# Block two makes all its own low parts, in a new order of projections and attention

## The reference

```python
h = rms_norm_2(x, attn_norm_g[l])
proj = h @ w_in[l]                       # 1024 x 3656
(mq, mk, mv, dq, dk, dv, sq, sk, sv, iq, ik, iw) = jnp.split(proj, offsets, axis=-1)
moba = moba_attention(qk(mq), qk(mk), mv)          # 4 heads, causal here
diff = diff_attention(dq 1 and 2, dk 1 and 2, dv, lam)   # 4 heads, v twice as wide
diff = rms_norm_2(diff, diff_subln_g[l]) * (1.0 - lam_init)
dsa = dsa_attention(qk(sq), qk(sk), sv, rope(iq), rope(ik), iw)   # 4 heads
x = x + concat(moba, diff, dsa) @ w_out[l]
h2 = rms_norm_2(x, ffn_norm_g[l])
x = x + (silu(h2 @ w_gate[l]) * (h2 @ w_up[l])) @ w_down[l]
```

## Time and profile before

| | us |
|---|---|
| three runs | 1736.86, 1734.09, 1737.43 |
| median | 1736.86 |
| profiled execution | 1736.14 |
| its span | 1734.0 |
| TensorE busy | 1622.6 |
| VectorE busy | 1048.5 |
| ScalarE busy | 760.5 |

### The profile page before, as it was taken

The page is one execution under the profiler, slowest core; times in us unless marked ns, Lnnn a source line. Parts: engine busy times, 40 slices in busy tenths (PEclk is TensorE's granted clock), DMA queues, the critical chain, the costliest instruction groups (busy, mean ns, idle before and its releaser), DMA issues.

```text
span 1734.0 us, 23510 instructions
## 1 busy us (share of the span) xinstructions
PE 1622.6 (94%) x9246; PEld 1319.6 (76%) x9246; DVE 1048.5 (60%) x1599; ACT 760.5 (44%) x1278; POOL 112.4 (6%) x120
## 2 busy tenths in 40 slices
PE   6999999999999989989999998789999998799999
PEld 3865676787888877578988866579998766589997
DVE  3537654654664346666654566658884566668873
ACT  3435523543453224545544445435454455445442
POOL 1010000010000001000000111100000011100000
PEclk9999999999999989999999999889999999899999
DMA  9349323687772225747655774135555664145553
GB/s 360 114 140 318 109 91 118 204 295 247 278 262 97 86 73 148 245 160 257 179 191 185 232 233 160 62 98 182 183 184 192 213 206 146 51 133 183 182 185 119
DMA packets 193549, 307.93 MB, mean 178 GB/s; under 512 B 12753, under 2 KB 96737, under 8 KB 193313
## 3 DMA queue, kind: packets, MB, share of 16 engines
q1 hardware_dynamic: 186720, 283.86, 49.9%
q0 software_dynamic: 6496, 22.51, 3.7%
q10 hardware_dynamic: 224, 0.07, 0.0%
HBM read 288.62 MB, written 17.78 MB: 177 GB/s over the span
## 4 chain that ended last, share of the span: by engine, by line
PE 79%; DVE 11%; ACT 3%; issue 2%; DMA 2%; POOL 1%; SPq 0%; POOLq 0%; DVEq 0%; ACTq 0%
PE bank L1824 48%; PE pair_bank L1824 20%; PE bank L1884 2%; DVE w_lo L1330 1%; PE pair_bank L2065 1%; PE bank L2093 1%; DVE wide L1414 1%; PE bank L2076 1%; DMA raw<-in_w_ada 1%; ACT probs L1160 1%; POOL xrstd L901 1%; DVE neg_max L1646 1%; DVE variance L1474 1%; POOL rstd L867 1%; PE pair_bank L2111 1%
## 5 line engine op out<-in xcount | busy, mean ns | idle before, releaser
L1330 DVE TENSOR_TENSOR w_lo<-raw,w_hi 128x1024 fp32r<-128x1024 f32 x374 | 448.6, 1220 | 296.5 <-ACT w_hi L1022 294.2
L1022 ACT CAST w_hi<-raw 128x1024 fp32r<-128x1024 f32 (+1 forms) x406 | 417.9, 1044 | 387.6 <-PE bank L1824 300.6
L1824 PE MATMUL pair_bank<-act_hi,w_hi 128*128 128x256 f32 (+1 forms) x736 | 231.1, 314 | 11.6 <-DVE act_lo L1404 6.0
L1824 PE MATMUL pair_bank<-act_hi,w_lo 128*128 128x256 f32 (+1 forms) x736 | 227.6, 309 | 0.0
L1824 PE MATMUL pair_bank<-act_lo,w_hi 128*128 128x256 f32 (+1 forms) x736 | 227.5, 309 | 0.0
L1824 PE MATMUL bank<-w_hi,hid_hi 128*128 128x512 f32 x560 | 222.1, 397 | 3.9 <-DVE residual L1725 3.9
L1824 PE MATMUL bank<-w_hi,hid_lo 128*128 128x512 f32 x560 | 222.0, 396 | 0.0
L1824 PE MATMUL bank<-w_lo,hid_hi 128*128 128x512 f32 x560 | 221.8, 396 | 0.0
L1824 PE MATMUL bank<-w_hi,act_hi 128*128 128x512 f32 (+2 forms) x528 | 212.0, 402 | 4.2 <-DVE w_lo L1330 2.1
L1824 PE MATMUL bank<-w_lo,act_hi 128*128 128x512 f32 (+2 forms) x528 | 203.9, 386 | 0.0
L1824 PE MATMUL bank<-w_hi,act_lo 128*128 128x512 f32 (+2 forms) x528 | 203.2, 385 | 0.0
(11 more groups left out here) (230 smaller groups left out, 2149.2 us busy)
## 6 DMA issues: line engine op xcount, KB each, us to landing
raw<-in_w_mlp SPq DMA_DIRECT2D x128, 512.0 KB, 3.8
raw<-in_w_in SPq DMA_DIRECT2D x106, 512.0 KB, 4.5
raw<-in_w_ada SPq DMA_DIRECT2D x96, 512.0 KB, 5.7
raw<-in_w_gate SPq DMA_DIRECT2D x44, 512.0 KB, 3.5
raw<-in_w_up SPq DMA_DIRECT2D x44, 512.0 KB, 3.5
raw<-in_w_down SPq DMA_DIRECT2D x44, 512.0 KB, 3.5
raw<-in_w_out SPq DMA_DIRECT2D x32, 512.0 KB, 3.9
split_lo<-w_lo POOLq DMA_DIRECT2D x30, 512.0 KB, 4.6
```

The costliest lines, as they stand in the source:

```text
L1022: nc.scalar.copy(hi_of(i)[:, 0:w], raw[:, i % RAW, 0:w]).then_inc(hi_ready, 1)
L1330: nc.vector.tensor_tensor(w_lo[:, i % RAW, 0:w], raw[:, i % RAW, 0:w], hi_of(i)[:, 0:w].bitcast(F32), ALU.subtract).then_inc(lo_ready, 1)
L1824: ins = nc.tensor.matmul(o, a[x], b[y], start=first and i == 0, stop=True, skip_group_check=True)
```

## The change

- The early slots and all that belongs to them are gone: 32 loads, casts, subtractions and stores in the first MLP, 32 reloads in block two, SyncE's waits ahead of them. All 29 low parts of a layer are made in block two by VectorE.
- The eight column blocks are in the order dq, dk, iq, mv_ik, mqk, sqk, dv, sv (before: iq, mv_ik, dq, dk, dv, mqk, sqk, sv). The values of the differential heads come in slots 23 to 26.
- The differential attention steps are scored and weighed from step 11 on. Their mixes wait for dv and are put off to step 28 and the first list of w_out; their transposed weights are kept, each in a place of its own (`MIX_AT`). Moba's mixes come before them, those of dsa all together in the fifth list of w_out.
- VectorE's part of `logits` is an item of its own, `gather`, one step or more behind TensorE's part. The index logits are at steps 16 to 21 instead of 7 to 13, the search is at 21 to the first list of w_out instead of 14 to the third.
- The slots of w_out go in the order of k (0, 2, 4, 6) instead of 2, 4, 0, 6. The differential rows are turned in bank 7 instead of bank 2, in the third list of w_out instead of the first.

```diff
-EARLY_SLOTS = (1, 3, 5, 8, 10, 12, 14, 15, 17, 18, 20, 21, 23, 24, 26, 28)
-EARLY_AT, EARLY_EVERY, BEHIND = 10, 1, 3
-EARLY = [(l, s) for l in range(DEPTH) for s in EARLY_SLOTS]
...
-        BLOCKS2 = (("iq", IQ), ("mv_ik", IK), ("dq", DQ), ("dk", DK), ("dv", DV), ("mqk", MQ), ("sqk", SQ), ("sv", SV))
+        BLOCKS2 = (("dq", DQ), ("dk", DK), ("iq", IQ), ("mv_ik", IK), ("mqk", MQ), ("sqk", SQ), ("dv", DV), ("sv", SV))
...
         FILL2 = {
             1: [("tables",)], 2: [("lam",)],
             3: [("drain", 0, 0), ("drain", 0, 1)],
-            4: [("first", 0), ("second", 0)],
-            5: [("first", 1), ("second", 1), ("turn", 0)],
-            6: [("drain", 1, 0), ("drain", 1, 1), ("turn", 1)],
-            7: [("first", 2), ("second", 2), ("index_scale",), ("turn", 2), ("logits", 0)],
-            8: [("logits", 1)],
-            9: [("logits", 2)],
-            10: [("drain", 2, 0), ("drain", 2, 1), ("logits", 3)],
-            11: [("first", 3), ("logits", 4)],
-            12: [("second", 3), ("first", 4), ("turn", 3)],
-            13: [("second", 4), ("turn", 4), ("logits", 5)],
-            14: [("drain", 3, 0), ("drain", 3, 1), ("search", 0, 3)],
-            15: [("first", 5), ("search", 0, 1)],
-            16: [("second", 5), ("first", 6), ("turn", 5)],
-            17: [("second", 6), ("turn", 6), ("score", 0)],
-            18: [("drain", 4, 0), ("weigh", 0), ("drain", 4, 1), ("search", 0, 2), ("score", 1)],
-            19: [("weigh", 1), ("mix", 0), ("search", 0, 2), ("score", 2)],
-            20: [("weigh", 2), ("mix", 1), ("search", 1, 1), ("score", 3)],
-            21: [("weigh", 3), ("mix", 2), ("search", 1, 1), ("score", 4)],
-            22: [("drain", 5, 0), ("weigh", 4), ("mix", 3), ("drain", 5, 1), ("score", 5)],
-            23: [("weigh", 5), ("mix", 4), ("first", 7), ("score", 6)],
-            24: [("weigh", 6), ("mix", 5), ("second", 7), ("square", 0), ("first", 8), ("turn", 7), ("score", 7)],
-            25: [("weigh", 7), ("mix", 6), ("second", 8), ("turn", 8), ("norm", 0), ("score", 8)],
-            26: [("drain", 6, 0), ("weigh", 8), ("mix", 7), ("drain", 6, 1), ("search", 1, 1), ("score", 9)],
-            27: [("weigh", 9), ("mix", 8), ("first", 9), ("square", 1), ("score", 10)],
-            28: [("drain", 7, 0), ("weigh", 10), ("mix", 9), ("drain", 7, 1), ("second", 9), ("first", 10), ("norm", 1), ("turn", 9), ("score", 11)],
+            4: [("first", 0)],
+            5: [("second", 0), ("first", 1), ("turn", 0)],
+            6: [("second", 1), ("turn", 1)],
+            7: [("drain", 1, 0), ("drain", 1, 1)],
+            8: [("first", 2)],
+            9: [("second", 2), ("first", 3), ("turn", 2)],
+            10: [("second", 3), ("turn", 3)],
+            11: [("drain", 2, 0), ("drain", 2, 1), ("score", 0)],
+            12: [("weigh", 0), ("score", 1), ("first", 4), ("second", 4)],
+            13: [("turn", 4), ("weigh", 1), ("score", 2), ("first", 5), ("second", 5)],
+            14: [("turn", 5), ("drain", 3, 0), ("weigh", 2), ("drain", 3, 1), ("score", 3)],
+            15: [("weigh", 3), ("score", 4), ("first", 6), ("second", 6), ("index_scale",)],
+            16: [("turn", 6), ("weigh", 4), ("score", 5), ("logits", 0)],
+            17: [("weigh", 5), ("score", 6), ("gather", 0), ("logits", 1)],
+            18: [("drain", 4, 0), ("weigh", 6), ("drain", 4, 1), ("score", 7), ("gather", 1), ("logits", 2)],
+            19: [("weigh", 7), ("gather", 2), ("logits", 3), ("first", 7)],
+            20: [("gather", 3), ("logits", 4), ("second", 7), ("first", 8)],
+            21: [("turn", 7), ("gather", 4), ("logits", 5), ("second", 8), ("search", 0, 1)],
+            22: [("drain", 5, 0), ("turn", 8), ("drain", 5, 1), ("score", 8), ("gather", 5), ("search", 0, 3)],
+            23: [("weigh", 8), ("score", 9), ("first", 9)],
+            24: [("mix", 8), ("weigh", 9), ("score", 10), ("second", 9), ("search", 0, 2)],
+            25: [("mix", 9), ("turn", 9), ("weigh", 10), ("score", 11), ("first", 10), ("search", 0, 2)],
+            26: [("drain", 6, 0), ("mix", 10), ("weigh", 11), ("drain", 6, 1), ("second", 10), ("search", 1, 2)],
+            27: [("mix", 11), ("turn", 10), ("score", 12), ("search", 1, 3)],
+            28: [("mix", 0), ("mix", 1), ("mix", 2), ("mix", 3), ("drain", 7, 0), ("weigh", 12), ("drain", 7, 1), ("score", 13),
+                 ("square", 0), ("search", 1, 2)],
         }
         OUT2 = {
-            0: [("weigh", 11), ("mix", 10), ("second", 10), ("turn_rows", 0), ("turn", 10), ("turn_rows", 1), ("score", 12)],
-            1: [("weigh", 12), ("mix", 11), ("search", 1, 2), ("score", 13)],
-            2: [("weigh", 13), ("search", 1, 3), ("mix", 12), ("score", 14)],
-            3: [("weigh", 14), ("mix", 13), ("score", 15)],
-            4: [("weigh", 15), ("mix", 14)],
-            5: [("mix", 15)],
+            0: [("mix", 4), ("mix", 5), ("mix", 6), ("mix", 7), ("weigh", 13), ("square", 1), ("search", 1, 1), ("score", 14)],
+            1: [("norm", 0), ("weigh", 14), ("norm", 1), ("score", 15)],
+            2: [("turn_rows", 0), ("turn_rows", 1), ("weigh", 15)],
+            4: [("mix", 12), ("mix", 13), ("mix", 14), ("mix", 15)],
         }
-        for x in range(len(EARLY)):
-            FILL["mlp1", 0].setdefault(EARLY_AT + x * EARLY_EVERY, []).append(("early", x))
...
-                return [(0, 2), (0, 4), (1, 2), (1, 4), (0, 0), (1, 0), (0, 6), (1, 6)]
+                return [(0, 0), (1, 0), (0, 2), (1, 2), (0, 4), (1, 4), (0, 6), (1, 6)]
...
+        MIX_AT = ((0, 0), (0, 1), (0, 2), (0, 3), (1, 0), (1, 2), (2, 0), (2, 2),
+                  (3, 0), (3, 2), (4, 0), (5, 0), (3, 0), (3, 2), (4, 0), (5, 0))
...
+            place, first = MIX_AT[j]
+            return (probs_t2[:, place] if place < 4 else mix_more[:, place - 4])[:, first:]
...
-                self.known_low(self.i - BEHIND)
...
-            def known_low(self, i):
-
-                if i < 0 or n.slots[i][0] != "known":
-                    return
-                x, r, u = n.value["known", i], i % RAW, n.slots[i][1]
-                was = n.value["early", x]
-                self.e.wait_ge(lo_stored[was % RAW], 16 * n.at(f"lo_stored{was % RAW}", was))
-                self.e.wait_ge(hi_ready, n.at("hi_ready", i))
-                self.e.dma_start(w_lo[:, r, 0:u].bitcast(F32), split_lo[x, :, 0:u]).then_inc(lo_loaded[r], 16)
-                n.put(f"lo_loaded{r}", i)
...
-            def early(self, x):
-                i = n.value.get(("early", x), 0)
-                u = n.slots[i][1]
-                self.e.wait_ge(lo_ready, n.at("lo_ready", i))
-                self.e.dma_start(split_lo[x, :, 0:u], w_lo[:, i % RAW, 0:u].bitcast(F32)).then_inc(lo_stored[i % RAW], 16)
-                n.put(f"lo_stored{i % RAW}", i)
...
-                if j >= MIXES:
-                    e.wait_ge(mixed, n.at("mixed", (key, j - MIXES)))
+                if j >= 12:
+                    e.wait_ge(mixed, n.at("mixed", (key, j - 4)))
...
-                if i >= len(n.slots) or n.slots[i][0] in ("ada", "known"):
+                if i >= len(n.slots) or n.slots[i][0] == "ada":
...
-            def logits(self, l, g):
+            def gather(self, l, g):
...
-                if n.slots[self.i][0] == "known":
-                    r = self.i % RAW
-                    self.e.wait_ge(hi_ready, n.at("hi_ready", self.i))
-                    self.e.wait_ge(lo_loaded[r], 16 * n.at(f"lo_loaded{r}", self.i))
-                else:
-                    self.e.wait_ge(lo_ready, n.at("lo_ready", self.i))
+                self.e.wait_ge(lo_ready, n.at("lo_ready", self.i))
...
-                u = units2(key[1])[(6, 6, 8, 10)[st["group"]]]
+                u = units2(key[1])[(3, 3, 8, 10)[st["group"]]]
...
-                if j == 0 or st["group"] != self.steps[j - 1]["group"]:
+                if j % 4 == 0:
                     for t in range(TT):
                         e.wait_ge(drained, n.at("drained", ("rows2", l, BLOCK2["dv" if st["diff"] else "mv_ik" if st["group"] == 2 else "sv"], t)))
-                    if st["group"] in (1, 2):
-                        e.wait_ge(diff_drained, n.at("diff_drained", (l, st["group"] - 1)))
+                    if st["group"] == 0:
+                        e.wait_ge(mix_lo, n.at("mix_lo", (key, 2)))
+                    elif st["group"] == 1:
+                        e.wait_ge(diff_drained, n.at("diff_drained", (l, 0)))
                     elif st["group"] == 3:
-                        e.wait_ge(mix_lo, n.at("mix_lo", (key, 2)))
+                        e.wait_ge(mix_lo, n.at("mix_lo", ("diff", l, 1)))
                 for kt in range(keys):
...
-                self.turn_bank()
+                if t == 0:
+                    e.wait_ge(diff_drained, n.at("diff_drained", (l, 1)))
+                else:
+                    e.wait_ge(mix_lo, n.at("mix_lo", ("diff", l, 0)))
                 for j in range(2):
```

(2 more changed lines are left out.)

76 lines of the change are left out of this document (23 added, 53 removed).

## The result

The changed kernel takes **1744.9 us** (median of 5 runs, 1744.3 to 1747.1), against 1737.4 for the kernel before, beside it on the same chip. The ratio is 1.0051 with a 95% interval of 1.0037 to 1.0064: slower, by half a per cent. (One of the five runs of before was disturbed and took 3159 us; it counts in the median of 1737.4, not in the ratio.) The prediction was 1745 in a range of 1717 to 1757.

A forecast was written before the change was run, and what follows sets the result against it. Block two's attention stages were taken as bound by a TensorE-VectorE round trip in middle and close. Per layer 39.3 + 94.1 + 47.0 + 1.0 = 181.4, +7.1; twice 14.3 less 5.6 = +8.7; 1736.1 + 8.7 = 1745 us, range 1717 to 1757.

The forecast's parts named there:

- Part 1: First MLP, end of its first column half: losing 32 early slots removes a wait and slow matmuls, 5.6 us gained once.
- Part 2: Block two: 16 more low parts per layer in VectorE's queue, 18.4 us per layer on its 110.1.
- the comparison of busy lists: Middle of the stage: VectorE's lists against TensorE's work, 27.9 to 28.8 us in slots 12 to 18, 51.6 to 41.0 after.
- Opening: Block two's stage, slots 0 to 11 and score 0: 39.3 us, bounds 38.5 to 41.
- Middle: Block two's stage, slots 12 to 28: 79.5 us of VectorE lists plus 15 handovers of 0.97, 94.1 us.
- (15.6 - 5.0) / 11: Price of a handover: VectorE's idle time in the old middle less waits for exponentials, over 11 steps, 0.97 us each.
- VectorE over 85% busy between slots 19 and 28: Sign named for the new order in block two, its idle time put down to the mask matmuls.
- Close: Block two's stage, behind the middle to the end of w_out: 47.0 us against 50.8, bounds 43 to 50.8.
- rival B: Gains and losses cancel: stage 1 to 4.5 us longer, paid by the first MLP's 5.6; 1733 to 1739, chance 0.16.
- Clock: Wait of some 4 us before weighing 11, at slot 26, lowers TensorE's clock: 1 us more per layer.
- A: Rival: VectorE finds work during handovers, stage 166 us, total 1714, or 1728 with half hidden; chance 0.27.
- The page's rule: Work first on the engine with highest occupancy; with TensorE 87% and VectorE 63% busy, 18 us on VectorE would be free.

The follow-up runs named there:

- e4_skip: The kernel before with its 32 early slots kept, but none at steps 19 to 24 of the first MLP; 1730.4 us, ratio to before 0.9957.
- e3_order: The kernel before with the changed kernel's order of blocks and steps, early slots kept; 1736.3 us, ratio to before 0.9999.
- e1_light: The changed kernel with 16 low-part subtractions per layer over 8 columns instead of 1024; 1730.5 us, ratio to before 0.9964.
- e5_hand: The changed kernel with one gather or search round moved ahead of the score in steps 17, 18, 24, 25 and 28; 1733.5 us, ratio to before 0.9985.
- e7_spread: The changed kernel with w_out's lists spread, so slots stand between the last scores and weighings; 1733.6 us, ratio to before 0.9981.
- e2_inplace: The kernel before with its order but no early slots, all low parts made in block two; 1738.7 us, ratio to before 1.0010.

## Why the prediction was right, point by point

**The result** came at 1744.9 for 1745, but two terms were off in opposite directions, and the loss was 7.7 us per layer in the mean (6.8 and 8.6) where 7.1 was written. The direction follows from the mechanism, VectorE's load and the handovers; that the number came out to 0.1 us is luck. In the trace the gain ahead of block two was 8.1 for 5.6, the two layers lost 15.4 for 14.3, and 1.5 came behind them for nothing.

**Part 1**: right, and shown. 5.66 us for 5.6 in the trace of after; e4_skip gets 6.6 from the same place alone, with all early slots kept. The store and reload traffic was rightly priced at nothing: e3_order, which has it, has no wait for it in its opening. e1_light has neither the traffic nor the load and takes 1730.5, e3_order 1736.3: the difference of 5.8 us is the column half's 5.6, and nothing is left for the traffic.

**Part 2**: the load was right, 126.3 and 127.9 us for 128, 36 subtractions of layer two in the window for 37. That it is paid is shown by e1_light, 7.2 us per layer. Where it is paid was not what the text said. It named slots 19 to 28 as the place where VectorE is the longer one; the dear low parts are those in the lists between score 0 and score 7 (steps 12 to 18), where VectorE had 24.9 us in 37.1 against 31.4 of TensorE and was not the longer. From score 7 to 13, the place that it named, only half of a low part is paid. The step of the prediction that failed is the comparison of busy lists, 27.9 for VectorE against 28.8 for TensorE, as a sign of where VectorE's work is paid; the sum itself charged every low part from slot 12 on in full, which is too much, 5.7 and 7.3 us measured for 8 x 1.15 = 9.2. Between scores 0 and 7 neither engine is full; a slot, its weighing, the next score and its maximum follow each other, and a subtraction in that ring adds most of itself.

**Opening**: 38.2 and 38.3 us for 39.3 at score 0, 0.2 to 0.3 below the lower bound of 38.5. A block of four slots took 13.5 and 13.1 where 13.9 was written.

**Middle**: 100.0 for 94.1 + 1.0, inside the bounds of 88.5 to 100.5, and both factors wrong. The lists were priced at 79.5 and are 74.1. The handovers were priced at 15 x 0.97 = 14.6 us; VectorE's idle time is 26.0, of which 13 waits for the mask make 21.2, 1.6 each. The two errors, -5.4 and +11.4, half cancel. The step that failed is (15.6 - 5.0) / 11: it spread VectorE's idle time of the old middle over all 11 steps. (It also took off too much: of the 5.0 us of waits for exponentials only 3.9 lie in that window. The 15.6 us of that window were 6.6 in five waits for the mask, 3.9 for exponentials, 3.7 for the mixed rows and 1.6 for the norm of the differential rows.) The trace of before has the wait by itself, from slot 18 to the end of the stage:

```profile
DVE neg_max L1646 <- PE pair_bank L2114: 11.1, 7, 3.0
```

7 waits of 1.6 us in the mean (0.16 to 2.95), the same mean as after. It was not shorter, it happened 7 times in place of 16: at the other nine maxima the mask was there before VectorE, which had other work in between. At the maximum of 1459.26, for one, it came straight from a first half and waited for nothing. That is what e5_hand gives back. So "VectorE over 85% busy between slots 19 and 28" was wrong: 45.3 of 58.75 us, 77%, from slot 19 to score 13.

**Close**: 45.0 for 47.0, against 50.8 before. From score 13 to score 14 it took 11.3 for 13.5. The two lists with no slot between them, named against rival B, do cost: e7_spread gets 5.3 to 5.6 us per layer by putting slots there.

**Clock**: the wait of about 4 us before weighing 11 is there, 4.18 at 1481.08, and the clock behind it, in the windows of 4 us:

```profile
1480.00:1484.00 4.00, 2.92 (x14) 2.95 (x15) 3.83 (x12) 1.80 (x3) 0.00 (x0) 0.50 0.00 0
1484.00:1488.00 4.00, 4.00 (x28) 3.50 (x26) 0.63 (x1) 0.70 (x2) 0.00 (x0) 0.72 0.00 1
1488.00:1492.00 4.00, 3.33 (x30) 3.16 (x30) 3.08 (x9) 2.69 (x8) 0.00 (x0) 1.00 0.35 131
```

0.50 is the level of 1.2 GHz. It stood for the 4 us in which matmuls began again and for half of the next 4; 1 us was the price written, and no run separates it from the wait.

**The rivals.** A (handovers hidden) was false for these lists, and true as a mechanism: e5_hand hides five of them and gains 4.4 and 5.3 us per layer. The condition that the text gave for A, that VectorE finds work during every handover, depended in these five steps on the order within one list. B fell, since the stage lost 6.8 to 8.6. The page's rule (Trainium skill, Perfetto Trace Analysis, Identifying the Most-Contended Engine: work first on the engine with the highest occupancy) was read too simply in the prediction. The same section says to judge TensorE's headroom by MFU and by the busy time of its weight loads, and not by that of its matmuls. The weight loads are busy for 115.3 of 174.5 us in rows 2, 66% beside VectorE's 63%, nearly level. So the rule called 18 us on VectorE free only by the 87% of the matmuls, a figure that the section tells readers not to use. e2_inplace's middle is a case where free would be right (4.3 us more on VectorE, and no longer), e1_light's first window one where it is wrong (4.2 us less, and 4.9 shorter, 1.5 of it the clock). VectorE was busy for 73% of the first in before (43.15 of 58.76) and for 67% of the second in after (24.93 of 37.10): in these two windows VectorE's occupancy does not tell which work is free.
